# Two attention mixers of a transformer kernel: small products and splits placed between projection tiles, and one input moved into the weight stream

## The reference, cut to what matters

```python
for i in range(2):
    h = 0.5 * swiglu(x, ffn1_w_gate[i], ffn1_w_up[i], ffn1_w_down[i])
    x = layer_norm(ALPHA * x + h, ...)
    h = hybrid_mixer(x, w_in[i], ...)            # the mixer
    x = layer_norm(ALPHA * x + h, ...)
    ...                                          # a second ffn with its norm
    x = x + sigmoid(x @ ple_w_gate[i] + ple_b_gate[i]) * (p[i] @ ple_w_proj[i])   # "ple"
# hybrid_mixer: proj = x @ w_in, split into three kinds of heads
q  = rope(nsa_q);  k_slc, k_win = rope(kv[2]), rope(kv[4]);  dq, dk = rope(diff_q), rope(diff_k)
compress(kv, pe, w1, w2):  blk = kv[:, idx] + pe;  return gelu(blk @ w1) @ w2     # 15 blocks of 32 tokens
kc = rope(compress(k_cmp, ...));  vc = compress(v_cmp, ...)
p_c = masked_softmax(q @ kc.T * scale);  o_cmp = p_c @ vc       # the compressed softmax
# and softmax attention over k_slc, k_win (nsa heads), dq/dk (diff heads), fox_q/fox_k (fox heads)
return concatenate([o_nsa, o_diff, o_fox]) @ w_out
```

## Time and profile before

| | us |
|---|---|
| runs of before | 3126.61, 3127.12, 3130.42 (median 3127.12) |
| profiled execution: span | 3127.4 |
| its PE busy | 2965.4 (95%) |
| its DVE / ACT busy | 1637.2 / 1291.8 |
| mixer of layer 0: end of the norm to its last projection product | 220.8 to 295.4 |
| mixer of layer 1: last projection product | 928.9 |

### The profile page before, as it was taken

The page is one execution under the profiler, slowest core; times in us unless marked ns, Lnnn a source line. Parts: engine busy times, 40 slices in busy tenths (PEclk is TensorE's granted clock), DMA queues, the critical chain, the costliest instruction groups (busy, mean ns, idle before and its releaser), DMA issues.

```text
span 3127.4 us, 51125 instructions
## 1 busy us (share of the span) xinstructions
PE 2965.4 (95%) x17586; PEld 2533.1 (81%) x17586; DVE 1637.2 (52%) x3043; ACT 1291.8 (41%) x2519; POOL 167.0 (5%) x121
## 2 busy tenths in 40 slices
PE   7999899999998999999999878999999999989998
PEld 7978789799797897788886545788878888768998
DVE  5565765555647656533335796433335333448554
ACT  4444445455544455432332444323324323335553
POOL 0000010000010100000000670000000000000000
PEclk9999899999998999999999988999999999989999
DMA  7555265555652656533333762333314233241553
GB/s 256 184 163 199 72 202 178 174 183 182 181 161 69 220 179 177 172 108 95 104 97 114 256 223 81 121 95 96 105 54 139 92 106 98 81 143 50 175 181 98
DMA packets 239052, 443.10 MB, mean 142 GB/s; under 512 B 26400, under 2 KB 27424, under 8 KB 238240
## 3 DMA queue, kind: packets, MB, share of 16 engines
q1 hardware_dynamic: 237344, 432.94, 44.1%
q0 software_dynamic: 1536, 7.86, 0.8%
HBM read 439.65 MB, written 1.05 MB: 141 GB/s over the span
## 4 chain that ended last, share of the span: by engine, by line
PE 82%; DVE 12%; issue 2%; POOL 2%; ACT 1%; DMA 1%; SPq 0%; DVEq 0%; POOLq 0%; ACTq 0%
PE ps L736 81%; DVE low L1720 1%; DVE hidden L1723 1%; POOL hidden L2306 1%; DVE zl L1723 1%; DMA raw<-weights 1%; DVE ps L1723 1%; DVE hidden L1720 1%; DVE zl L1720 1%; DVE coef L2228 1%; DVE hidden L2232 1%; POOL low L2276 1%; DVE gated L1720 1%; DVE hidden L2055 0%; DVE neg_max L2028 0%
## 5 line engine op out<-in xcount | busy, mean ns | idle before, releaser
L736 PE MATMUL ps<-zh,low 128*128 128x256 f32 (+1 forms) x4192 | 1400.6, 334 | 79.1 <-DVE low L1720 41.1
L736 PE MATMUL ps<-zl,high 128*128 128x256 f32 (+1 forms) x4192 | 1381.8, 330 | 0.0
L736 PE MATMUL ps<-zh,high 128*128 128x256 f32 (+1 forms) x4192 | 1380.9, 329 | 0.0
L1720 DVE TENSOR_TENSOR low<-raw,high 128x512 fp32r<-128x512 f32 x1276 | 843.8, 699 | 462.1 <-ACT high L1277 460.3
L1277 ACT ACTIVATE high<-raw 128x512 fp32r<-128x512 f32 x1304 | 761.7, 625 | 572.6 <-PE ps L736 499.5
L736 PEld LDWEIGHTS ps<-zh,low 128*128 128x128 f32 x4192 | 806.0, 192 | 184.0 <-DVE low L1720 42.2
L736 PEld LDWEIGHTS ps<-zl,high 128*128 128x128 f32 x4192 | 806.7, 192 | 71.8 <-issue 4.8
L736 PEld LDWEIGHTS ps<-zh,high 128*128 128x128 f32 x4192 | 806.5, 192 | 69.1
L1720 DVE TENSOR_TENSOR hidden<-gated,ps 128x256 f32 (+1 forms) x176 | 91.5, 520 | 604.2 <-ACT gated L1277 604.2
L1277 ACT ACTIVATE gated<-ps 128x256 f32<-128x256 f32 (+1 forms) x176 | 81.3, 462 | 497.3 <-PE ps L736 497.1
L736 PE MATMUL ps<-high,zl 128*128 128x512 f32 (+2 forms) x544 | 195.2, 359 | 3.8 <-DVE zl L1720 3.8
(11 more groups left out here) (190 smaller groups left out, 2016.8 us busy)
## 6 DMA issues: line engine op xcount, KB each, us to landing
raw<-weights SPq DMA_DIRECT2D x1640, 256.0 KB, 3.4
hidden<-norms POOLq DMA_DIRECT2D x4, 1024.0 KB, 7.0
cst<-consts SPq DMA_DIRECT2D x1, 1829.0 KB, 14.3
x<-x_in SPq DMA_DIRECT2D x1, 1024.0 KB, 7.0
x<-tokens_in POOLq DMA_DIRECT2D x1, 1024.0 KB, 13.8
x<-ctx_in POOLq DMA_DIRECT2D x1, 1024.0 KB, 6.4
out<-hidden POOLq DMA_DIRECT2D x1, 1024.0 KB, 5.1
ple_p<-p_in POOLq DMA_DIRECT2D x1, 512.0 KB, 7.2
```

Source lines behind the costliest of these rows:

```text
L736: return nc.tensor.matmul(out, lhsT, rhs, start=first, stop=last, **kw)
L1720: return nc.vector.tensor_tensor(out, a, b, op)
```

## The change

1. `stream()`: the 16 raw compress quarters, in one block behind the values before, are cut into four groups of 4, placed behind tiles 3, 5, 7 and 9; the two `phi2` quarters come behind the three value groups, and tiles 10 to 17 behind the last values.
2. PE's mixer follows this order: pair 1, phi(0), pair 2, swap, phi(1), pair 3, swap, phi(2), pair 4, swap, phi(3), values, swap, `sel32` product, values, transposes, values, `phi2` products, last values, swap of kc, pair 5, compressed scores, pair 6, transposes, pairs 7 and 8, the products with `vc_diag`, then the attention scores. All of it uses the same instructions and sizes as before; PSUM banks differ.
3. ACT and DVE follow: rope, splits, forget gates and compressed softmax stand between their splits of weights. The four fox pairs (tiles 10 to 17) are rounded and subtracted straight out of PSUM, without a copy in `proj`. The rounded roped tiles go to `h_split`, half of their low parts to a new buffer `q_low`.
4. ple: `p` of the layer comes as a fifth raw quarter in the weight stream; the POOL transfer of `ple_p` (512 KB) at the start is gone.

```diff
@@ stream()
-        yield from (("tile", ("w_in", l), t, 2, t == T_FORGET) for t in range(2, 18))
+        for t in range(2, 10, 2):
+            yield from (("tile", ("w_in", l), i, 2, i == T_FORGET) for i in (t, t + 1))
+            yield ("phi", l, t // 2 - 1, 4, True)
         yield from (("values", ("w_v", l), t, 4, False) for t in range(3))
+        yield ("phi2", l, 0, 2, True)
         yield ("tile", ("w_v", l), 6, 2, False)
-        yield ("phi", l, 0, 16, True)
-        yield ("phi2", l, 0, 2, True)
+        yield from (("tile", ("w_in", l), t, 2, False) for t in range(T_FQ, 18))
@@ PE.mixer
+                pair(1, 1)
+                pe.wait_ge(blocks_ready, seen(blocks_ready, 2))
+                phi(0)
+                self.fills_out()
+                pair(2, 2)
+                pe.wait_ge(proj_ready, pr0 + 2)
+                swap(T_KSLC, "swap64", 4)
+                phi(1)
+                pair(3, 3)
+                pe.wait_ge(proj_ready, pr0 + 3)
+                swap(T_NQ, "swap64", 5)
+                phi(2)
+                pair(4, 0)
+                pe.wait_ge(proj_ready, pr0 + 4)
+                pe.wait_ge(rope_ready, ro0 + 1)
+                swap(T_DQ, "swap32", 4)
+                phi(3)
+                self.values(ps[:, 1, :], range(ST))
...
+                pe.wait_ge(val_ready, seen(val_ready, 4))
+                pair(7, 0)
+                pair(8, 3)
+                pe.wait_ge(cmp_t, seen(cmp_t))
                 for t in range(ST):
                     m = self.mm(ps[:, 7, t * 256:t * 256 + 256], pc_t[:, t, :], vc_diag[:], True, True)
...
-                pe.wait_ge(qk_low, seen(qk_low, 8))
+                pe.wait_ge(qk_low, lo0 + 7)
...
                     if first == 2:
                         pe.wait_ge(cmp_taken, l + 1)
+                        pe.wait_ge(qk_low, seen(qk_low, 8))
@@ Act.mixer
+                for n in range(5):
                     self.used(4)
...
+                    if n == 2:
+                        act.wait_ge(forget_in, seen(forget_in))
+                        self.f(fl[:, 0, :], fl[:, 3, :], ACT.Abs).then_inc(act_step, 1)
...
+                        self.f(lam_s[:, 0:2], lam_s[:, 0:2], ACT.Exp).then_inc(lam_act, 1)
+                    if n >= 3:
+                        roped(n - 3)
...
+                foxes(2, 0)
+                foxes(3, 3)
                 self.fill(7, 4)
                 self.ahead(-5)
@@ Dve.mixer (its end)
+                self.used(4)
+                foxes(2, 0)
+                self.used(4)
+                lows_of(T_DQ, 3)
+                lows_of(T_DK, 4)
+                foxes(3, 3)
                 while self.s < self.q + KT + 3:
                     self.low()
                 v.wait_ge(tokens_ready, self.norms - self.norms // 3)
@@ PE.ple
-                        w = self.raw_quarter()
...
-                            m = self.mm(y_tile(S, d), w[:, i * P:i * P + P], ple_p[:, l, k, :], ...)
+                            m = self.mm(y_tile(S, d), w[2 * k + a][:, i * P:i * P + P], p[:, k * S:k * S + S], ...)
@@ gpsimd
-            pool.dma_start(ple_p[:], p_in).then_inc(rest_landed, 16)
```

More of the change, by code:

```diff
@@ L980, in mixer, with pair @@
                 coming = self.coming_input(S)
[L981 to L989, removed]
-                        continue
+                pr0, va0, ro0, lo0 = seen.now(proj_ready), seen.now(val_ready), seen.now(rope_ready), seen.now(qk_low)
+                def pair(n, bank):
                     for d in range(2):
-                        o = ps[:, n % 4, d * S:d * S + S]
+                        o = ps[:, bank, d * S:d * S + S]
                         if 2 * n + d != T_FORGET:
@@ L1007, in mixer, with swap, phi @@
                         self.done(m)
[L1009 to L1013 removed]
+                def swap(t, name, bank):
+                    self.mm(ps[:, bank, :], c(name), proj[:, t:t + 2, :], True, True).then_inc(swapped, 1)
+                def phi(part):
+                    for n in range(4 * part, 4 * part + 4):
+                        w = self.raw_quarter()
+                        for i in range(2):
+                            at = 32 * (2 * (n % 2) + i)
+                            m = self.mm(ps[at:at + 32, 6, 0:HID], block_kv[:, 2 * n + i, :], w[:, i * HID:i * HID + HID], n < 2, n >= CMP_BLOCK // 2 - 2,
+                                        skip_group_check=True)
+                        self.done(m)
@@ new lines, in mixer @@
+                self.values(ps[:, 2, :], range(ST))
+                pe.wait_ge(gelu_ready, seen(gelu_ready))
+                for h in range(2):
+                    m = nc.tensor.transpose(ps[:, 6, 2 * NC * h:2 * NC * h + 2 * NC], hid_r[:, h * P:h * P + P], c("ident", slice(0, 2 * NC))[:, 0:2 * NC])
+                m.then_inc(hid_turned, 1)
+                self.values(ps[:, 3, :], range(ST))
+                two = [self.raw_quarter(), self.raw_quarter()]
+                wk, wv = two[0][:, 0:256].rearrange("p (h m) -> p h m", h=2), two[1][:, 0:128].rearrange("p (h m) -> p h m", h=2)
@@ L1457, in mixer, with roped, foxes @@
                 self.take_rows()
-                for n in range(9):
+                ro0 = seen.now(rope_ready)
+                seen(rope_ready, 4)
+                def roped(n):
+                    act.wait_ge(rope_ready, ro0 + n + 1)
+                    self.f(r(high_at(ROPED[n], 2)), proj[:, ROPED[n]:ROPED[n] + 2, :], ACT.Copy).then_inc(qk_high, 1)
+                def foxes(n, bank):
+                    self.used(4)
+                    self.f(r(high_at(FOXES[n], 2)), ps[:, bank, :].rearrange("p (a s) -> p a s", a=2), ACT.Copy, scale=PROJ_SCALE[5 + n]).then_inc(qk_high, 1)
+                for n in range(5):
                     self.used(4)
@@ L1484, in mixer @@
+                roped(2)
+                self.used(4)
+                act.wait_ge(hid_turned, seen(hid_turned))
+                self.f(hid[:].rearrange("p a b -> p (a b)"), ps[:, 6, 0:4 * NC], ACT.Copy).then_inc(hid_ready, 1)
+                roped(3)
                 act.wait_ge(forget_ready, seen(forget_ready))
```

219 lines of the change are left out of this document (114 added, 105 removed).

## The result

| | before | after |
|---|---|---|
| runs | 3126.61 to 3130.42, median 3127.22 | 3094.14, 3098.15, 3099.07, 3105.27, median 3098.61 |
| ratio after / before, 95% interval | | 0.991, 0.9896 to 0.9924 |
| profiled execution, span | 3127.4 | 3103.2 |

Predicted were 3097.0 us, in a range from 3090 to 3108. The changed kernel was run in two more sets: 3096.81 (ratio 0.9913) and 3098.53 (0.9903). All 13 of its executions lie between 3092.6 and 3105.3, with a median of 3098.15.

The account below looks back on a forecast made before the run. PE was taken to bound the kernel, 95% busy, leaving only its idle spells and slow clock to gain. 2 x (13.0 mixer + 1.5 jobs) + 1.3 start = 30.3 us off 3127.4 gave 3097 us, range 3090 to 3108.

Parts of the forecast that it names:

- The mechanism: Both mixers: small products move from a poor stretch into the dense projections at full clock, saving 13.0 us per layer.
- The point E: Moment PE ends the mixer's last tile, predicted 11.4 us after the dense work's former end at 295.44.
- small products and switches: In the mixer: swaps 3.6 us, compress products 4.0, other small products 3.3, changes between dense and small work 0.5.
- the clock inside the dense stretch: Assumed full at no cost; rival: small products halve it and the kernel is slower, 3137 at 20 us' worth, chance 0.04.
- The tail: DVE's chain from the last tile to the first attention maximum: low parts, fox pair, weight splits, compressed output; 4.8 us.
- The jobs: Attention jobs behind the mixer: better clock at their start saves 1.5 us per layer, half of a practical 3.
- The start: Kernel start: without the 512 KB ple transfer PE's third weight quarter lands 1.3 us earlier, all of it counting.
- the ple stage: The ple bytes come hidden behind 8 gate quarters; cost 0, up to 0.5 us, with the 2.27 us DVE wait there already.
- Not fully hidden: Rival: ring or forget chain makes PE wait at the compress groups, 1 to 4 us a layer, 3099 to 3105; chance 0.20.
- the step with the margin of 0.7 us: ACT's forget chain ends at 247, before pair 4's splits; cost 0, or 1 to 2 us a layer if late.
- The ring: Weight buffer slots, freed when PE has used raw quarters, refill in time between compress groups; cost 0.
- the prediction's bound: Upper bound for weight-ring waits, one in each of the four compress groups: 4 us a layer.

Follow-up runs that it names:

- forget_apart: Changed kernel with the forget tile's 8-column products and two halves of its 12-column products placed between other tiles; median 3093.84 us, ratio 0.990 to before.
- no_gates: Changed kernel with two 24-column products in place of the gates' 32 products of 12 columns; 3096.22 us.
- the three kernels with the tile apart: Changed kernel with the forget tile split up: alone 3093.84 us, with a shortened tail 3091.41, and with tile 7's weights also split before the forget chain 3091.92.
- after_again: Second repeat of the changed kernel, code unchanged; 3098.53 us, ratio 0.9903.
- ple_only: Kernel before with only the ple input moved into the weight stream, mixers unchanged; 3123.69 us, ratio 0.9995 to before.
- forget_first: Changed kernel with tile 3 (forget products) ahead of tile 2; 3106.29 us, ratio 0.9942, 9.5 us slower than the changed kernel.
- short_tail: Changed kernel with vc_diag products ahead of pair 8, nsa jobs before diff jobs, and DVE's work behind the last tile cut; 3090.17 and 3089.08 us.

## Why the prediction was right, and where not

The time (3098.6 for 3097.0) and the order of the terms were right; the sum was closer than its parts.

**The mechanism** held: the dense stretch takes in all small products, no wait for transfers or the forget chain is left, and a compress group at full clock costs 1.07 us (predicted 1.0).

**The point E.** The prediction puts it 11.4 us behind the dense work's length, 70.1 + 11.4 = 81.5 us from the first forget product (225.32 to 295.44 before). In after it is 85.25 (224.75 to 310.00) and 83.71 (845.20 to 928.91), of which 0.2 is DVE's start behind PE's (309.80 to 310.00). Without a low clock it is 83.75 in forget_apart with a wait of 1.44, so 82.3; in no_gates 80.18, less 1.0 of waiting, plus the 3.1 left out, again 82.3. So small products and switches were 0.6 too cheap, and the rest, 1.4 to 2.9 us, goes with the low clock.

**The step that failed** is the clock inside the dense stretch, which the sum holds at 1.00 and at a cost of nothing. I had a rival for it, but priced it only from 15 us on, and set against it the 13 us before 222 and the 1.00 in layer 0. Layer 1 of the same trace had the answer; these are its stretches in the kernel before:

```profile
857.00:865.00 8.00, 8.00 (x56) 5.67 (x55) 1.95 (x6) 0.89 (x4) 5.21 (x3) 1.00 0.07 29
865.00:869.00 4.00, 4.00 (x23) 4.00 (x22) 3.65 (x2) 3.31 (x7) 4.00 (x2) 0.57 0.60 208
869.00:928.00 59.00, 59.00 (x497) 59.00 (x496) 25.47 (x40) 27.88 (x49) 0.15 (x1) 1.00 0.58 183
```

The fall was there before the change, in one layer of two. Of the 18 whole forget tiles in nine profiles, 15 have a low stretch behind them; of the 8 in no_gates and the three kernels with the tile apart none has. In after phi(0) lies in it, at nearly twice its price. The clock explains the layers. Mixer 0 saved 8.3 us and mixer 1 15.5, while the time that PE was busy at the low clock fell by 0.7 us in the first (17.7 to 17.0) and by 15.5 in the second (25.7 to 10.2); half of that difference is 7.4 us. Behind the forget products the low stretches are 6.8 us in mixer 0 (none before) and 3.4 in mixer 1 (3.4 before). The rest lies at the jobs and behind them: after has one of 3.4 us at 371.0 in mixer 0, before has one at 1015.6 in mixer 1. Why it is 3.4 us in one execution and 6.8 in the next stays open.

**The tail** of 4.8 us was 4.4 in both layers. From first forget product to first maximum there are 89.65 and 88.10 us, against 99.35 and 100.83 before: 9.7 and 12.7 saved where 13.0 was predicted; in the repeats 11.2 and 12.7, 7.9 and 11.2.

**The jobs** (1.5 us a layer) were the step trusted least. From the first to the eighth maximum layer 0 took 11.52 us for 11.76, layer 1 11.16 for 12.39: 0.2 and 1.2. In the second repeat, with 10.2 us at the low clock, these were 12.26 and 12.16 us, so nothing was gained. In after the clock is full for their first 2.0 and 0.9 us, then falls. By the page "TensorE: Matmul & The Clock Gate" of the Trainium skill (section "HAM oscillation — how this bites in real kernels") only idle gaps of some length re-throttle the array. The runs do not agree, as far as PE's rows can tell: behind the 12-column products it fell with no idle time between the rows.

**The start** was right at its place (17.63 for 19.07, predicted 1.3), and so was the ple stage: its wait of 2.27 us is at 624.89, as at 635.53 before. How much of the start's gain arrives is not shown.

**The rivals.** *Not fully hidden* did not come in the profile of after, but the stretch has little to spare: in after_again PE waited 2.08 us for the block additions, which the prediction does not name, and with tile 7 right behind the forget chain, the step with the margin of 0.7 us, a wait of 1.44 came. The ring had slack with four raw quarters in a row. With sixteen, mixer 1 took 9.3 us more (194.2 for 184.9): 4.0 us are idle time of PE, which is the prediction's bound, and 4.5 are half of the 9.0 us more at low clock. The Trainium skill ("ScalarE: Activation LUTs", section "What ACT_TABLE_LOAD costs") has a drain beside each table load. It does not show in forget_apart either: load at 238.18, 1.28 long, next activation at 239.48.

**The sum.** The mixers gave 23.8, 25.2 and 17.2 us in three executions; 29 was predicted. The four stages behind them together gave some 5 us in each execution that I had not forecast, 2.8 to 7.9 in the eleven profiled executions with the new mixers and 0.4 with the ple input alone. By the table of idle time and clock this is less of both: 2.0 us less idle and 6.5 less at low clock in after make 5.2 us, where 5.1 were measured. In the ffn2 stage of layer 0 the clock was low for 6.8 us before and not at all in the three executions of after. Why the clock falls less often there stays open. The stage with GpSimd's splits gave between -4.4 and +4.7, by scatter. And the 29 was set against one profile of before, whose mixer 0 was 5.6 us shorter than the same code in ple_only. That the median fell within 1.6 us of the forecast is therefore partly luck.

## What to carry to other kernels

Small products between dense tiles cost what they cost at full clock where the clock holds, and their buffers decide how many may stand in a row: four raw quarters were free, sixteen were not. Before moving work, read the granted clock in every repetition of the stage, since a fall in one layer of two is a price that both may pay. Compare stages by idle time and by time at low clock, and not by length alone, since the second differs between executions of the same code. And ask of each instruction near the change what hides it now: the forget products hid the block additions, and putting tile 3 first, which set a split that waited for a ring slot in front of them, cost 9.5 us.

## What the runs showed of the hardware that was not expected

- PE, with no idle time between its rows (whose durations include the tail of the pipeline), went from 1.00 to 0.50 behind 32 products of 12 columns (3.7 us), for 3.4 or 6.8 us; the 16 products with 8 output rows before them (3.6 us) did not do it by themselves in the two layers of no_gates. In two halves, with 2.9 us of dense products between, they did no harm.
- The two block additions on DVE took 2.00 us while POOL was idle, and 3.88 and 6.01 us in two executions in which it worked on the tokens; there one addition took 2.9 to 3.1 us where 0.95 to 1.0 is usual. A weight split took 2.91 us beside POOL in forget_first where 0.69 is usual. DVE's durations beside a working POOL are no constants. The page "SBUF — State Buffer" of the Trainium skill (section "Who interferes with whom") has DVE instructions with two inputs in SBUF contend with a POOL instruction that reads SBUF, the loser waiting for the whole instruction; the block additions have two such inputs, and these rows agree.
- Executions of the same code differ by 12 us in the stage in which POOL makes a part of the splits, 179.8 to 192.2 us; PE's waits for POOL's splits were 15.9 and 13.3 us at one end (forget_apart, and forget_first with 180.1), 20.5 (short_tail) and 21.2 (after, 189.6 us) at the other.
